# Second feed-forward's last 64 gate and value columns as one unit, and bias with row maximum, multiplicities with row sum, as single VectorE instructions

## What is computed

```
for l in range(2):
    x = x + mixer1(rms_norm(x)) @ w_out[l]        # rope attention, differential attention, gated scan
    gate, val = split(rms_norm(x) @ w_up[l])      # 2816 columns each
    x = x + (gelu(conv3(gate)) * val) @ w_down[l]
for layer in range(2):
    x = x + 0.5 * swiglu(rms_norm(x), w_gate, w_up, w_down)    # D_FF_2 = 2752 columns each
    x = x + even_mixer(...) or odd_mixer(...)
    x = x + 0.5 * swiglu(rms_norm(x), w_gate, w_up, w_down)

def swiglu(x, w_gate, w_up, w_down):
    return (silu(x @ w_gate) * (x @ w_up)) @ w_down
```

## Time and profile before

| | |
|---|---|
| median of 3 runs | 1765.04 us (1764.23 to 1765.81) |
| the profiled execution's own time | 1760.74 us |
| its span, first to last instruction | 1759.0 us |
| TensorE matmul busy | 1676.2 us, 95% |
| VectorE busy | 1235.6 us, 70% |
| ScalarE busy | 945.0 us, 54% |
| GpSimd busy | 514.8 us, 29% |
| mean granted TensorE clock | 0.980 |
| HBM read | 272.09 MB |

### The profile page before, as it was taken

How to read it: one execution, slowest core, us unless ns; L and a number is a source line. 1 busy time by engine, 2 the same in 40 slices (tenths; PEclk the granted TensorE clock), 3 DMA queues, 4 the chain that set the end, 5 groups by cost and what they waited for, 6 DMA issues and landing times. The chain is left out here.

```text
span 1759.0 us, 30432 instructions
## 1 busy us (share of the span) xinstructions
PE 1676.2 (95%) x10338; PEld 1461.1 (83%) x10338; DVE 1235.6 (70%) x1942; ACT 945.0 (54%) x1553; POOL 514.8 (29%) x492
## 2 busy tenths in 40 slices
PE   7896999999987999999999989999999999899999
PEld 6785899988866999888889857888888889578887
DVE  5776777757786777667766867776577766967764
ACT  5454566544553666456645555665466534456652
POOL 0040433310312433134421004443144411444430
PEclk9998999999997999999999999999999999999999
DMA  6330456645321566556664304656565654236563
GB/s 251 103 114 25 129 182 188 216 164 156 103 66 60 170 183 210 190 167 184 199 197 154 121 13 127 186 189 207 164 187 184 218 178 154 83 123 189 188 215 99
DMA packets 71066, 274.15 MB, mean 156 GB/s; under 512 B 7888, under 2 KB 9040, under 8 KB 70992
## 3 DMA queue, kind: packets, MB, share of 16 engines
q1 hardware_dynamic: 70992, 273.17, 49.0%
HBM read 272.09 MB, written 1.05 MB: 155 GB/s over the span
## 5 line engine op out<-in xcount | busy, mean ns | idle before, releaser
L810 DVE TENSOR_TENSOR wl<-raw,wh 128x1024 fp32r<-128x1024 f32 (+1 forms) x474 | 624.1, 1317 | 127.1 <-ACT wh L529 120.6
L529 ACT ACTIVATE wh<-raw 128x1024 fp32r<-128x1024 f32 (+1 forms) x474 | 529.9, 1118 | 223.7 <-PE gb L1223 126.5
L1219 PE MATMUL gb<-hx,wh 128*128 128x512 f32 x1540 | 553.8, 398 | 0.0
L1220 PE MATMUL gb<-hx,wl 128*128 128x256 f32 x1540 | 432.2, 281 | 0.0
L1219 PE MATMUL gb<-gux,wh 128*128 128x512 f32 x960 | 341.2, 394 | 0.0
L1219 PEld LDWEIGHTS gb<-hx,wh 128*128 128x128 f32 x1540 | 289.8, 188 | 60.5
L1206 PE MATMUL gb<-hx,wh 128*128 128x256 f32 x1008 | 298.0, 296 | 17.5 <-DVE hx L827 9.9
L1220 PEld LDWEIGHTS gb<-hx,wl 128*128 128x128 f32 x1540 | 291.0, 189 | 7.9
L1207 PE MATMUL gb<-hx,wh 128*128 128x256 f32 x1008 | 287.0, 285 | 0.0
L1208 PE MATMUL gb<-hx,wl 128*128 128x256 f32 x1008 | 286.6, 284 | 0.0
L1220 PE MATMUL gb<-gux,wl 128*128 128x256 f32 x960 | 268.1, 279 | 0.0
(11 more groups left out here) (203 smaller groups left out, 2101.1 us busy)
## 6 DMA issues: line engine op xcount, KB each, us to landing
raw<-in_wa SPq DMA_DIRECT2D x378, 512.0 KB, 3.5
raw<-in_wb SPq DMA_DIRECT2D x96, 704.0 KB, 4.2
x<-in_x SPq DMA_DIRECT2D x2, 512.0 KB, 5.8
out_x<-x SPq DMA_DIRECT2D x8, 128.0 KB, 3.1
row<-in_row SPq DMA_DIRECT2D x1, 836.0 KB, 10.9
tab<-in_bias SPq DMA_DIRECT2D x3, 256.0 KB, 4.5
con<-in_const SPq DMA_DIRECT2D x1, 544.0 KB, 7.9
tab<-in_bias SPq DMA_DIRECT2D x1, 512.0 KB, 5.3
```

What stands on the lines that cost most here:

```text
L529: nc.scalar.activation(wh[:, slot, 0:nt * P], raw[:, slot, 0:nt * P], ACT.Copy).then_inc(s_hi, 1)
L810: nc.vector.tensor_tensor(wl[:, slot, 0:nt * P], raw[:, slot, 0:nt * P], wh[:, slot, 0:nt * P].bitcast(f32), ALU.subtract).then_inc(s_lo, 1)
L1219: nc.tensor.matmul(bank[:, :], a, both(k), start=start and k == 0, stop=False)
L1220: nc.tensor.matmul(bank[:, 0:SEQ], b, high(k), start=False, stop=False)
```

## The change

Two edits that don't touch each other.

**Feed-forward 2.** The 64 left-over gate columns and the 64 left-over value columns are laid side by side as one unit, so that an ffn2 phase has 43 up units, and 59 in all where it had 60. The gate stands on partitions 0 to 63 of the bank `gb[2]` and the value on 64 to 127. A branch `both` in `up` handles this pair: ScalarE makes two copies of 64 partitions, both before its `ahead(0)`; there is no `ahead(1)`. The hidden block 21 keeps 128 partitions; its upper half holds what an earlier pair left and meets zero rows of `w_down`. The loops of ffn2 run one trip less and pairs 18 to 21 are written out.

**Softmax on VectorE.** L959 and L962 become one `tensor_tensor_reduce` for each half of 256 columns, which writes (table + scores) x bias and its maximum; L977 and L978 become one for each half, which writes the product and its sum. Since the instruction scales the sum of both inputs, the differential heads' scores must be divided by the bias beforehand: eight small VectorE instructions at the program's start put the query gain over the bias to `bqs`, and the query normalisation reads that.

```diff
-                    link(nc.vector.scalar_tensor_tensor(out=pr[:, r % 6, :], in0=tab[:, 0:512], scalar=h.bias,
-                                                        in1=s, op0=ALU.mult, op1=ALU.add))
-                    s = pr[:, r % 6, :]
-                link(nc.vector.reduce_max(small[:, 16 + o:18 + o], pair(s), axis=AX.X))
+                    for qt in range(2):
+                        cs = slice(qt * SEQ, (qt + 1) * SEQ)
+                        last = nc.vector.tensor_tensor_reduce(out=pr[:, r % 6, cs], in0=tab[:, cs], in1=s[:, cs], scale=h.bias,
+                                                              scalar=LOWEST, op0=ALU.add, op1=ALU.max,
+                                                              accum_out=small[:, 16 + o + qt:17 + o + qt])
+                    link(last)
+                else:
+                    link(nc.vector.reduce_max(small[:, 16 + o:18 + o], pair(s), axis=AX.X))
...
-                    link(nc.vector.tensor_tensor(pr[:, r % 6, :], pr[:, r % 6, :], tab[:, 512:1024], ALU.mult))
-                    link(nc.vector.reduce_sum(sums, pair(pr[:, r % 6, :]), axis=AX.X))
+                    for qt in range(2):
+                        p1 = pr[:, r % 6, qt * SEQ:(qt + 1) * SEQ]
+                        last = nc.vector.tensor_tensor_reduce(out=p1, in0=p1, in1=tab[:, 512 + qt * SEQ:512 + (qt + 1) * SEQ], scale=1.0,
+                                                              scalar=0.0, op0=ALU.mult, op1=ALU.add,
+                                                              accum_out=sums[:, qt:qt + 1])
+                    link(last)
...
+UP = {"ffn1": 2 * FC, "ffn2": 2 * FC - 1}
...
+                    if both:
+                        act.wait_ge(s_pe, i + 1)
+                        nc.scalar.activation(low[0:HALF, j, 0, :], gb[2 * j][0:HALF, SEQ:2 * SEQ], ACT.Copy).then_inc(s_gl, 1)
+                        nc.scalar.activation(low[HALF:P, j, 1, :], gb[2 * j][HALF:P, SEQ:2 * SEQ], ACT.Copy).then_inc(s_vl, 1)
+                        ahead(0)
+                        act.wait_ge(s_gs, p + 1)
+                        nc.scalar.activation(tap[0:HALF, j, :], gs[0:HALF, j, 1:SEQ + 1], ACT.Silu).then_inc(s_tap, 1)
+                        act.wait_ge(s_gu, p + 1)
+                        nc.scalar.activation(guh[:, ds(it * (2 * SEQ) + j * SEQ, SEQ)], gu[:, j, :], ACT.Copy).then_inc(s_guh, 1)
+                        return
...
+                    if both:
+                        gate, t = gs[0:HALF, j, 1:SEQ + 1], tap[0:HALF, j, :]
+                        dve.wait_ge(s_gl, it * 2 + (B0[n] + j + 1))
+                        nc.vector.tensor_tensor(gate, gb[2 * j][0:HALF, 0:SEQ], low[0:HALF, j, 0, :], ALU.add).then_inc(s_gadd, 1)
+                        dve.wait_ge(s_gadd, it * 2 + (B0[n] + j + 1))
+                        nc.vector.tensor_tensor(gate, gate, rstd[0:HALF, :], ALU.mult).then_inc(s_gs, 1)
+                        ahead(0)
+                        dve.wait_ge(s_gul, p - 1)
+                        dve.wait_ge(s_vl, p + 1)
+                        nc.vector.tensor_tensor(gu[0:HALF, j, :], gb[2 * j][HALF:P, 0:SEQ], low[HALF:P, j, 1, :],
+                                                ALU.add).then_inc(s_vadd, 1)
+                        dve.wait_ge(s_up, p + 1)
+                        dve.wait_ge(s_vadd, p + 1)
+                        nc.vector.tensor_tensor(gu[0:HALF, j, :], gu[0:HALF, j, :], t, ALU.mult).then_inc(s_gu, 1)
+                        return
```

More of the change, by code:

```diff
@@ L24 @@
 IN_UNITS = {"mix1": 26, "even": 14, "odd": 16}
-UNITS = {"mix1": 26 + 8, "even": 14 + 8, "odd": 16 + 8, "ffn1": 2 * FC + 16, "ffn2": 2 * FC + 16}
+UNITS = {"mix1": 26 + 8, "even": 14 + 8, "odd": 16 + 8, "ffn1": 2 * FC + 16, "ffn2": 2 * FC - 1 + 16}
+UP = {"ffn1": 2 * FC, "ffn2": 2 * FC - 1}
+HALF = P // 2
 M1_AQ, M1_AK, M1_AV, M1_CQ, M1_CF, M1_CB, M1_CG, M1_CV, M1_BV, M1_B = 0, 3, 4, 5, 7, 9, 11, 13, 15, 18
@@ L117, in k_tiles @@
         n = max(n for n in range(NPH) if U0[n] <= i)
-        return KD if not is_mix[n] and i - U0[n] >= 2 * FC else DC
+        return KD if not is_mix[n] and i - U0[n] >= UP[PHASES[n][0]] else DC
     ctx = ExitStack()
@@ L150, in build_program @@
         small = sb("small", [P, 96])
+        bqs = small[:, 88:96]
         with ExitStack() as turn:
@@ L394, in _ @@
                 else:
-                    with sp.Fori(0, FC // 2) as it:
+                    with sp.Fori(0, UP[kind] // 4) as it:
                         for j in range(4):
@@ L704, in feed_forward, with up @@
                 F, C, U, conv = F0[n], G0[n], U0[n], kind == "ffn1"
-                def up(it, j, last):
+                def up(it, j, last, both=False):
                     p, i = it * 2 + (F + j), it * 4 + (U + 2 * j)
@@ L855, in start_values @@
                 for l in range(2):
+                    for h in heads("mix1"):
+                        if h.bias is not None:
+                            nc.vector.tensor_scalar(bqs[:, 4 * l + h.h:4 * l + h.h + 1], col("bq", l), 1.0 / h.bias, None, ALU.mult)
                     lam0 = 0.8 - 0.6 * math.exp(-0.3 * l)
@@ L867, in head_norm @@
                 for k, (name, at0) in enumerate(gains):
-                    ins = nc.vector.scalar_tensor_tensor(out=yc(c + k), in0=yc(c + k), scalar=col(name, at0),
+                    gain = col(name, at0) if name != "bq" else bqs[:, 4 * l + (c - M1_B) // 2:4 * l + (c - M1_B) // 2 + 1]
+                    ins = nc.vector.scalar_tensor_tensor(out=yc(c + k), in0=yc(c + k), scalar=gain,
                                                          in1=sq[:, k * SEQ:(k + 1) * SEQ], op0=ALU.mult, op1=ALU.mult)
@@ L1169, in down @@
                     ahead(1)
-                for one, trips in ((up, FC // 2 - 1), (down, 3)):
+                whole = UP[kind] // 4 - 1
+                for j in range(2):
+                    up(0, j, False)
+                with dve.Fori(1, whole) as it:
                     for j in range(2):
-                        one(0, j, False)
-                    with dve.Fori(1, trips) as it:
-                        for j in range(2):
-                            one(it, j, False)
+                        up(it, j, False)
+                for p in range(2 * whole, FC):
+                    up(p // 2, p % 2, True, 2 * p + 2 > UP[kind])
+                for j in range(2):
+                    down(0, j, False)
+                with dve.Fori(1, 3) as it:
                     for j in range(2):
-                        one(trips, j, True)
+                        down(it, j, False)
+                for j in range(2):
+                    down(3, j, True)
             split_next(0)
@@ L1454, in feed_forward, with up @@
                 F, U = F0[n], U0[n]
-                def up(it, j, first):
-                    for k in range(2):
+                def up(it, j, first, units=2):
+                    for k in range(units):
                         i = it * 4 + (U + 2 * j + k)
@@ L1472, in feed_forward @@
                     up(0, j, True)
-                with pe.Fori(1, FC // 2) as it:
+                with pe.Fori(1, UP[kind] // 4) as it:
                     for j in range(2):
                         up(it, j, False)
+                for p in range(UP[kind] // 4 * 2, FC):
+                    up(p // 2, p % 2, False, min(2, UP[kind] - 2 * p))
                 def down(it, j, first):
                     for k in range(2):
-                        b = U + 2 * FC + 2 * j + k
+                        b = U + UP[kind] + 2 * j + k
                         if not first and k == 0:
@@ L1507, in up_units @@
 def up_units(gate, val):
-    g, v = units_of(gate), units_of(val)
-    return np.stack([g, v], 1).reshape(2 * g.shape[0], P, -1)
+    whole = gate.shape[1] // P * P
+    g, v = units_of(gate[:, :whole]), units_of(val[:, :whole])
+    units = np.stack([g, v], 1).reshape(2 * g.shape[0], P, -1)
+    if whole < gate.shape[1]:
+        units = np.concatenate([units, units_of(np.concatenate([gate[:, whole:], val[:, whole:]], 1))], 0)
+    return units
 def down_units(w):
```

20 lines of the change are left out of this document (12 added, 8 removed).

## The result

| | before | after |
|---|---|---|
| median | 1764.63 us (1763.22 to 1765.81, 4 runs) | 1738.85 us (1736.68 to 1739.54, 4 runs) |
| profiled execution, span | 1760.74, 1759.0 us | 1739.11, 1737.3 us |

The ratio is 0.9852, 95% interval 0.9837 to 0.9868: 25.8 us quicker, where the forecast had 20.7 and a lower end of 1740.5 us. Between the two profiled executions the difference is 21.6 us.

A forecast was written before the change was run, and what follows sets the result against it. TensorE was taken to bound ffn2, VectorE a stretch of odd and some heads elsewhere. Units 11.3, odd 4.6, even 1.6 and mix1 3.2 sum to 20.7 us: 1765.0 to 1744.3 us, 80% range 1740.5 to 1753.0.

The forecast's parts named there:

- the row instructions' terms: Softmax rows in odd, even and both mix1 phases: one-instruction pairs save 4.6, 1.6 and 3.2 us, 9.4 in all.
- Units, 11.3 us: Four ffn2 phases: one unit less saves 2.82 us each, 11.3 in all; the merged unit's chain keeps 0.15 to 0.75 cover.
- Rival 1: ffn2: the merged pair's chain is late, costing at most 3.4 us in all, giving 1747.7 us; chance 10%.
- Price of a pair, 1.03 us: VectorE softmax: a fused pair takes 1.03 us instead of 1.43, saving 0.40 (0.09 to 0.46).
- Rival 2, half rate: Odd's sums: the form with two SBUF inputs runs at half rate, 1.55 us a pair, giving 1747.1 us; chance 18%.
- Odd, 4.6 us: Odd, the stretch bound by VectorE: quicker pairs save 2.4 + 1.4 + 0.8 = 4.6 us.
- can come forward by 2.4 us: Odd, first part of the bound stretch: TensorE's idle time of 1.4 + 1.0 us goes once VectorE is quicker.
- 1.4 + 0.8: Odd: 1.4 us of VectorE's lag at the last input unit goes, and two more pairs before the long wait's end give 0.8.
- Even, 1.6: Even: four table additions stand on the chain, 4 x 0.40 = 1.6 us saved.
- Mix1, 1.6 a phase: Both mix1 phases: two pairs ahead of each of two TensorE waits save 4 x 0.40 = 1.6 us a phase, 3.2 together.
- an uncertainty with no sign: Granted clock in two mix1, even and odd: where drops fall may move the time 3 us either way; nothing in the sum.
- rival 5: Whole kernel: a pair at 0.97 us and clock drops that fall well save 23.7 us, giving 1741.3 us; chance 15%.

The follow-up runs named there:

- the two chain runs: Changed kernel with two, then four, idle ScalarE copies of 1024 columns ahead of the merged unit's Silu: 1737.17 us, then 1748.74 us.
- the filled wait: Kernel before with four unread 256-column matmuls on TensorE ahead of the 2.7 us wait in both mix1 phases: 1760.94 us, ratio 0.9985.

## Why the forecast missed, step by step

The forecast was too small by 3.0 us in the phases, and the 3.6 us of busy time that the clock gave back there (sum of the table's row before rounding) are more than that; the forecast's sum had the clock at nothing. TensorE's idle time in the mixing phases fell by 8.8 us where the row instructions' terms had 9.4. That this agrees is luck: a pair saved 0.64 and not 0.40, with which the forecast's own count (twelve pairs in mix1 and even, and 2.4 + 1.4 + two pairs in odd) would give 12.8. Price and count were both off, and the two errors nearly cancel.

- **Units, 11.3 us: right.** Term, mechanism (TensorE alone bounds ffn2) and cover held. Rival 1 did not come; the two chain runs show that it was near, with 0.8 us of cover and 2 us a phase beyond it.
- **Price of a pair, 1.03 us: too high**, and its lower bound, 0.97, as well. The bound added the read's 0.08 to the 0.34 between two mains. The rows show read and next main starting together; only the last read of a pair counts. The Trainium skill, VectorE: DVE Perf Modes, "Two Vector instructions with no wait between them", says that an instruction with an accumulator output is two, a main one and a read. The trace agrees (x64 of each on L983); that the read is free of cost in front of another main, only the trace shows.
- **Rival 2, half rate: wrong.** 256 columns from two SBUF operands take 0.42 us, no more than from PSUM (0.41). The Trainium skill's rule, Vector Engine (DVE) Microarchitecture Reference, "7. Points that are easy to get wrong", is not borne out for this instruction; the measurement decides. Whether the instruction is of the family that the rule names stays open. The kernel before had one that is, without an accumulator: the scalar-tensor-tensor of L868, 128 x 256 with both inputs in SBUF, has a median of 0.479 us (37 of them), against 0.424 for L1163 with one input in PSUM. That instruction stood in the trace before and was not among the rows that the forecast used.
- **Odd, 4.6 us: measured 3.7.** The step that TensorE "can come forward by 2.4 us" was right: the waits of 1.4 and 1.0 are gone. Of the 1.4 + 0.8 behind it only 1.3 came: a wait of 0.8 at the last input unit is gone, and the long wait fell from 3.9 to 3.4 us, not to about 2. At 0.64 for each of 15 pairs VectorE would have had 9.6 us less to do; its busy time fell by 6.4, in part because the sums collide with GpSimd, and the phase by 3.7.
- **Even, 1.6: measured 1.0.** The first output unit came earlier by 1.3 us. TensorE's idle time fell by 2.0, and the clock took 0.9 of it back.
- **Mix1, 1.6 a phase, and the clock put at no sign: the step that failed.** The waits fell from 2.7 and 1.6 to these (second mix1 after):

```profile
PE mb L1392 <- DVE mx L1055: 1.5, 1, 1.5
...
PE mb L1364 <- DVE small L993: 0.7, 1, 0.7
```

  That is 2.1 us where 1.6 was forecast, the pair's price again. The other 3.4 to 3.5 are the clock: with the shorter wait the lower level ended near 522 and not at 534. The forecast saw the drop and put the clock down as "an uncertainty with no sign". In this stretch there was one. From the start of the phase, this stretch at the lower level ends after 138 us in the kernel before, in the units alone and in the sum alone, after 128 in every run with the quicker maxima and no added matmuls, and after 130 with the filled wait. (With seven and ten matmuls at the later wait its last part ends after 135 and 134.) In the first mix1 the idle time fell by 1.0 only, since the wait of 2.8 there did not get shorter. In odd and even the clock had no such sign: the changed kernel is at the lower level from 1515 to 1522 and from 1044 to 1054, the kernel before from 1534 to 1537 and from 1059 to 1063, and in its second profiled execution from 1534 to 1545 and from 1060 to 1067.
- **Profile and median.** Taking the sum off the median was right. With the terms corrected, 20.7 + 3.0 = 23.7 gives 1741.3 from 1765.04, the very figure of rival 5 (15%), which had a cheap pair and drops of the clock that fall well, and was right in kind; its 0.97 a pair was still too high, so that the figure itself is luck. The medians measured, 1738.85 and 1739.72, lie another 1.6 to 2.4 us lower; that is within what single executions of either kernel differ by, and no run says more about it.

## What to carry to other kernels

Where a stretch shows the lower granted clock just behind a wait of TensorE, count the wait's shortening twice: once as idle time, once as the work behind it that runs at the upper level; or fill the wait with matmuls that nobody reads, which was worth 12 us here, more than the 9.4 us that the row instructions were forecast to give. To see which of the two a change gave, take TensorE's busy time apart from its idle time, phase by phase. When two edits shorten the same chain, ask after the first how much idle time is left; the second edit can be worth nothing. And before trusting a thin cover, look for an instruction on it that is stretched by company on another engine: it will move with the schedule.

## What the runs showed of the hardware that was not expected

- GpSimd's product of 128 x 256 takes 0.73 us alone and 1.87 us when VectorE runs a split of 1408 columns beside it. It works the other way too. Timelines of VectorE and of GpSimd in odd:

```profile
1498.75 0.82 DVE L1005 CUSTOM_DVE_ANT_0 pr<-pr,tab 128x256 f32<-128x256 f32 x1
1499.50 0.94 DVE L1005 CUSTOM_DVE_ANT_0 pr<-pr,tab 128x256 f32<-128x256 f32 x1
```

```profile
1498.69 0.60 POOL L498 TENSOR_TENSOR at<-qq,con 128x240 f32<-128x240 f32 x1
1499.36 0.80 POOL L499 TENSOR_TENSOR at<-at,y 128x256 f32<-128x256 f32 x1
```

  The same instruction takes 0.42 us when GpSimd is idle. That makes the mean of 554 ns in its group. The form that reads PSUM shows no such thing: its mean is 416, and one at 1497.88 takes 0.41 beside a GpSimd product that runs from 1496.95 to 1498.43. The Trainium skill, SBUF — State Buffer, "Who interferes with whom", has one rule, that the port pair shared by VectorE and GpSimd is locked by one of them at a time. The trace agrees: both of these end 0.28 us after GpSimd's instruction, and GpSimd's product of 1.87 us ends 0.60 after VectorE's split, about as if each had waited for the other.
- The accumulator's read takes 0.08 us, and costs nothing when another main instruction follows: the two start together, and the mains stay 0.34 apart.
- Two ScalarE copies of 64 partitions, the second on the upper half, start 0.40 us apart, where a copy and a split of 128 started 0.28 apart.
- Granted clock below the full level moved the mixing phases of one and the same kernel by up to 1.8 us each between executions, and no ffn2 phase by more than 0.1.
